# Encoder trunk: the split of the fourth in-projection slab goes to another slot and one step sooner, and half of the out-projection's weights is loaded later

## The reference

```
mod = silu(c) @ mod_w[l] + mod_b[l]              # six parts of 1024: shift, scale, gate, twice
h = rmsnorm(x, g) * (1 + scale) + shift
z = h @ w_in                                     # 2560 columns: a_val, a_gb, a_gc, b_gate, b_in, 512 each
y_a = a_gb * conv3(a_gc * a_val)
xr = conv4(b_in) + b
h_rec = rglru(xr, forward) + rglru(xr, reverse)  # sigmoid gates, a = exp(...), linear scan over the sequence
y_b = gelu(b_gate) * h_rec
x = x + gate * (concat(y_a, y_b) @ w_out)
x = x + gate2 * grouped_moe(...)                 # 16 experts, top 2
...
```

## Time and profile before

| | |
|---|---|
| runs of the kernel | 1388.5, 1387.87, 1386.01 us; median 1387.87 |
| the profiled execution's own time | 1388.95 us |
| its span, first to last instruction | 1387.2 us |
| busy: PE, DVE, ACT, POOL | 1278.2, 1033.7, 680.4, 164.0 us |
| mean granted clock of PE | 0.969 |
| out-projection of layer 0 starts | 201.48 us |

### The profile page before, as it was taken

How to read it: one execution, slowest core, us unless ns; L and a number is a source line. 1 busy time by engine, 2 the same in 40 slices (tenths; PEclk the granted TensorE clock), 3 DMA queues, 4 the chain that set the end, 5 groups by cost and what they waited for, 6 DMA issues and landing times.

```text
span 1387.2 us, 15640 instructions
## 1 busy us (share of the span) xinstructions
PE 1278.2 (92%) x5389; PEld 907.8 (65%) x5389; DVE 1033.7 (75%) x1415; ACT 680.4 (49%) x877; POOL 164.0 (12%) x169
## 2 busy tenths in 40 slices
PE   2999899989999999996899999999799999999876
PEld 2466765577777777753788854468777777777532
DVE  8679975477898888837766587856678898888253
ACT  3477402326667666614222167644366667666002
POOL 6000000010000000010000057710100000000200
PEclk9999999899999999999999999999899999999989
DMA  9727674257999999885465230022689999998651
GB/s 353 243 91 273 227 264 190 91 212 279 379 384 378 389 384 388 323 320 212 134 235 180 89 122 0 1 77 99 278 312 392 389 381 381 385 381 321 234 198 60
DMA packets 78116, 347.84 MB, mean 251 GB/s; under 512 B 12500, under 2 KB 12684, under 8 KB 69104
## 3 DMA queue, kind: packets, MB, share of 16 engines
q1 hardware_dynamic: 67184, 325.70, 62.7%
q0 software_dynamic: 7344, 16.68, 3.2%
q10 hardware_dynamic: 3536, 4.79, 0.9%
HBM read 334.15 MB, written 23.07 MB: 258 GB/s over the span
## 4 chain that ended last, share of the span: by engine, by line
PE 73%; DVE 13%; DMA 6%; ACT 4%; issue 3%; POOL 1%; SPq 0%; DVEq 0%; POOLq 0%; ACTq 0%
PE ps L1968 24%; PE ps L2101 8%; PE ps L1994 8%; PE ps L2001 6%; PE ps L1879 4%; DVE scratch L1054 3%; PE ps L1886 3%; PE ps L1954 2%; PE ps L1846 2%; DMA mod_ring<-y_rows,y_row 2%; PE ps L2145 2%; PE ps L2173 2%; PE ps L2159 2%; DMA x_res<-in_x_dram 1%; PE ps L1841 1%
## 5 line engine op out<-in xcount | busy, mean ns | idle before, releaser
L1968 PE MATMUL ps<-slab_ring_r,gate_rows_r 128*128 128x512 f32 x512 | 200.8, 392 | 0.0
L1476 DVE TENSOR_TENSOR slab_ring_r<-slab_ring,h_t_r 128x2048 fp32r<-128x2048 f32 x64 | 143.7, 2284 | 5.3 <-ACT h_t_r L858 5.3
L2101 PE MATMUL ps<-slab_ring_r 128*128 128x512 f32 x384 | 120.0, 394 | 6.3 <-DVE h_t_r L1111 6.3
L858 ACT ACTIVATE h_t_r<-slab_ring 128x2048 fp32r<-128x2048 f32 x64 | 118.7, 1903 | 0.0
L1994 PE MATMUL ps<-slab_ring,scratch 128*128 128x512 f32 x256 | 116.9, 600 | 1.5 <-ACT scratch L900 1.5
L1968 PEld LDWEIGHTS ps<-slab_ring_r,gate_rows_r 128*128 128x128 f32 x512 | 97.1, 190 | 18.5
L1968 PE MATMUL ps<-h_t_r,gate_rows_r 128*128 128x512 f32 x256 | 104.3, 407 | 4.9 <-DVE slab_ring_r L1476 4.9
L1968 PE MATMUL ps<-h_t_r,scratch_r 128*128 128x512 f32 x256 | 101.4, 396 | 0.0
L725 POOL TENSOR_SCALAR mod_ring<-mod_ring,row_rcp 128x512 f32<-128x512 f32 x48 | 76.9, 1614 | 204.7 <-DVE row_rcp L1732 204.6
L1476 DVE TENSOR_TENSOR slab_ring_r<-slab_ring,x_norm_r 128x2048 fp32r<-128x2048 f32 x32 | 73.1, 2287 | 19.3 <-ACT x_norm_r L858 19.3
L1476 DVE TENSOR_TENSOR slab_ring_r<-slab_ring,mod_ring_r 128x2048 fp32r<-128x2048 f32 x32 | 73.1, 2287 | 19.3 <-ACT mod_ring_r L858 19.3
(11 more groups left out here) (360 smaller groups left out, 2710.3 us busy)
## 6 DMA issues: line engine op xcount, KB each, us to landing
slab_ring<-in_expert_w_gate_dram SPq DMA_DIRECT2D x35, 2048.0 KB, 8.6
slab_ring<-in_expert_w_up_dram SPq DMA_DIRECT2D x35, 2048.0 KB, 10.1
slab_ring<-in_expert_w_down_dram SPq DMA_DIRECT2D x35, 2048.0 KB, 10.3
mod_ring<-in_mod_w_dram SPq DMA_DIRECT2D x40, 512.0 KB, 4.7
y_rows<-scratch SPq DMA_DIRECT2D x32, 512.0 KB, 10.5
slab_ring<-in_mod_w_dram SPq DMA_DIRECT2D x32, 512.0 KB, 4.8
slab_ring<-in_mod_w_dram SPq DMA_DIRECT2D x12, 1024.0 KB, 11.3
slab_ring<-in_w_qkv_dram SPq DMA_DIRECT2D x6, 2048.0 KB, 17.0
```

Source lines behind the costliest of these rows:

```text
L858: act.activation(top, w, ACT.Copy).then_inc(high_ready[c], 1)
L1476: tt_(rest, w, top.bitcast(F32), ALU.subtract).then_inc(low_ready[c], 1)
L1968: ins = pe.matmul(ps[:, bank, :], x, w, start=(kt == 0 and i == 0), stop=(kt == KT - 1 and i == 2))
L2101: ins = pe.matmul(ps[:, i % 6, :], x[:, kt, cut], y[:, k, :], start=(kt == 0 and n == 0), stop=(kt == KT - 1 and n == 2))
```

## The change

The high parts of slab 3 go to slot 0 of the ring, which is free once slab 0's four tiles are done, and are made one tile step sooner on ACT, behind tiles j = 1 and j = 2 in place of 2 and 3. Slab 4's high parts keep `HT_r`, which they now share with slab 2 only. The low parts of slab 3 are moved ahead in DVE's list. Slot 0 is then taken until z tile 15, so the first out-projection slab is loaded later, behind the second.

```diff
@@ in_split_of
-        top = ring_r[:, 5, :, :] if g == 1 else HT_r
+        top = {1: ring_r[:, 5, :, :], 2: HT_r, 3: ring_r[:, 0, :, :], 4: HT_r}[g]
@@ SP
         load_mod(4)
-        load_slab(("out", 0), w_out[:, :, 0:HALF])
         load_mod(5)
         sp.wait_ge(z_ready, 12)
         load_slab(("out", 1), w_out[:, :, HALF:D])
+        sp.wait_ge(z_ready, 16)
+        load_slab(("out", 0), w_out[:, :, 0:HALF])
         load_mod(6)
@@ ACT, high_in
-            if g > 2:
-                act.wait_ge(z_ready, 4 * (g - 1) + 2 * half + 2)
+            if g == 3:
+                act.wait_ge(z_ready, 4)
+            if g == 4:
+                act.wait_ge(z_ready, 10 + 2 * half)
@@ ACT, end of tile step j
-            if j >= 2:
-                high_in(3, j - 2)
+            if j in (1, 2):
+                high_in(3, j - 1)
@@ DVE
         gates_in(2)
+        low_in(3, 0)
         mod_acc(3, 6, 2)
         gates_out(2)
-        low_in(3, 0)
         mod_acc(4, 0, 3)
         gates_in(3)
+        low_in(3, 1)
         mod_acc(4, 3, 2)
         gates_out(3)
-        low_in(3, 1)
         mod_acc(4, 5, 3)
```

## The result

The changed kernel takes 1391.55 us (median of 20 runs, 1387.83 to 1395.75), the kernel before 1387.86 (20 runs, 1384.79 to 1391.09). The ratio is 1.0019 with a 95% interval of 1.0011 to 1.0028, that is 2.6 us slower (1.5 to 3.9). The medians differ by 3.7 us. The change made the kernel a little slower, by an amount that lies at the line of 0.2%.

What follows compares the result with a forecast made beforehand. The prediction took DVE's arrival at low_in(4, 1), then a race between PE and DVE, as the bound. DVE's order (2.21 us) and the second slab (1.47) sum to 3.68, giving 1387.87 + 3.7 = 1391.5 us; range 1388.0 to 1393.8.

Steps and rivals of the forecast that it cites:

- the sum: Likeliest case: DVE's 2.21 us and the second slab's 1.47 add to 3.68 us; chance 0.55, 0.49 of it to slower.
- Part 1: ACT: slab 3's high parts one tile step sooner fit its 5.13 us idle time; cost nothing, gain nothing.
- Part 2: DVE: low_in(3, 0) ahead of gates_out(2) delays ACT's j = 3 step, so DVE waits longer for ACT; +2.21 us.
- Part 3: PE: tile 14 no longer waits, its 4.3 us hole goes to before tile 16; gain nothing.
- Part 4: Transfer queue: the second out-slab ahead of load_mod(6)'s slices makes DVE wait 2.1 us; +1.47 us at the out-projection.
- The unknown: PE's clock may fall after 2.3 us pauses before tile 18 and the out-projection; taken as nothing, upper bound 1.7 us.
- B: Rival: load_mod(6)'s slices are not held up by the second slab, only DVE's order costs; +2.2 us, 1390.1; chance 0.16.
- C: Rival: PE's clock falls before the out-projection (1393.3), or slab 3 lands late for ACT's j = 2 step (1393.8); chance 0.13.
- D: Rival: no effect; ACT's step does not hold DVE and the slices come in time; 1387.9; chance 0.09.
- E: Rival: faster; PE decides, tile 14's 4.3 us wait and the slow clock carry to tile 19; 6.0 us, 1381.9; chance 0.07.

Runs made afterwards that it cites:

- e3: Changed kernel with DVE's old order restored and one out-projection slab moved behind load_mod(6); ratio to the kernel before 1.0000 (0.9987 to 1.0013).
- e1: Changed kernel with DVE's list put back in the old order, loads as changed; ratio to the kernel before 0.9998 (0.9980 to 1.0016).
- e7: Changed kernel with low_in(3, 1) ahead of gates_in(3) in place of behind it; ratio to the kernel before 1.0007 (0.9989 to 1.0025).
- e2: Changed kernel with one out-projection slab ahead of load_mod(6) and the other behind it, DVE's order as changed; ratio to the kernel before 1.0003 (0.9987 to 1.0018).
- e6: Changed kernel with out-slab ("out", 0) issued from ACT's queue after z tile 15, not from SP; ratio to the kernel before 1.0006 (0.9991 to 1.0021).
- changed_again: The changed kernel once more, with no edit, for a second profile; ratio to the kernel before 1.0026 (1.0010 to 1.0042).
- e4: Changed kernel with e2's edit, low_in(3, 0) ahead of gates_in(2) and low_in(3, 1) ahead of gates_in(3); ratio to the kernel before 0.9988 (0.9971 to 1.0005).
- e5: e4 with six mod_acc products ahead of gates_in(0) and low_in(2, 0) ahead of gates_out(0); ratio to the kernel before 0.9963 (0.9946 to 0.9981).
- e8: e5 with low_in(4, 1) moved ahead of mod_acc(5, 6, 2) and val(3); ratio to the kernel before 0.9978 (0.9964 to 0.9991).
- e5_again: The kernel of e5 run a second time, with no edit; ratio to the kernel before 0.9986 (0.9971 to 1.0000).

## Why the prediction was right

**Result.** 1391.5 was forecast and 1391.55 measured. That the two agree to 0.05 us is luck: timed again, the changed kernel's median lay 4.7 us over that of the kernel before (1393.27 against 1388.56) and not 3.7. What supports the sum are the terms, read in the traces. The case with the largest chance, the sum, is what happened. The ratio with its interval puts the loss at 1.5 to 3.9 us, which holds the 3.68 of the sum, near its upper end, but also values on the other side of the 0.2% line. That split of the chances can't be called confirmed; the medians alone are on the slower side.

**Part 1** (sooner high parts cost nothing): right. The slab landed near 112.5 against 112.4, and e3 shows no cost.

**Part 2** (2.21 us by DVE's order): right. The traces show 2.15 at `low_in(4, 1)` in absolute time and 2.22 as a distance; e1 and e7 take it away, each in another way, and e2 shows it alone. The waits were forecast as 1.16 and 2.4, and are 1.20 and 2.38.

**Part 3** (PE's hole moves to before tile 16, no gain): right, and in e1 and e3, where the longest of PE's waits is 2.8 us, the first distance is that of before with its 4.3. One number was off: the pause before tile 18 was to be 2.3 us and was 1.17. Behind the longer hole tile 16 began at the lower clock (0.50 from 174 to 178 us, where before had 0.58), and tiles 16 and 17 took 13.85 us (174.88 to 188.73) where before's took 12.75. The forecast had not counted that. That ate a part of the pause and delayed nothing, since tile 18 waits for DVE.

**Part 4** (1.47 us by the second slab): right. DVE's wait was 2.10 (2.1 forecast), the third slice was used by 195.82 (195.76), and PE waited for the last `gb`. e1 measures the term alone as 1.49; e2 and e6 take it away.

**The unknown**, PE's clock before the out-projection: the pause was 2.35 us, and the granted clock from 205 to 209 was 1.00. Nothing was lost, as taken, and that was luck too. Four runs had a pause of nearly this length there: the changed kernel 2.35 us, changed_again 2.32 and e7 2.39 kept the clock at 1.00, and e1 with 2.27 lost it, and with it the 1.70 us that the prediction gave as its upper bound.

**Rivals.** B (the slices overtake) is refuted by the 14.4 us from issue to landing and by e2. That a later transfer may complete before an earlier one doesn't mean that a small one passes 4 MB ahead of it, and here none did. C asked for a lower clock behind 205 or for a slab landing at 117.6; neither is there in the changed kernel, but e1 shows that C's clock was a real risk. For D, ACT's step does hold DVE. E asked that `low_in(4, 1)` start no later than before. That was not so here; e4, e5 and e8 met its condition by another order of DVE, and there the out-projection starts 1.5 to 4.1 us sooner than before (e4's 115.17 and e8's 112.60 against 116.65). E's full 6.0 us came in none of them.

**The profiled execution** was to take 1392.6, with a span of 1390.9. Its span was 1394.0; the 3 us more lie behind the out-projection's start and did not come back in changed_again.

## What to carry to other kernels

When an engine splits its time between a chain that another engine answers (here DVE's scan, ACT's next gates) and work that only has to be done some time, put that work ahead of the wait for the answer, not between the last result and the signal that starts the answer: the same two low parts of 2.2 us each cost 2.2 us behind the gates (e2) and gained 1.5 us ahead of them (e4). Ask of a large load not only whether it is needed late enough, but which small ones stand behind it in the queue. A hole on an engine off the last chain was worth nothing here: the changed kernel, e1 and e3 moved or cut PE's hole and gained nothing by it.

## What the runs showed of the hardware that was not expected

Pauses of nearly one length had both outcomes for TensorE's clock. Eight matmuls of 512 columns, of the same line, took 5.37 us behind a pause of 2.50 us in e1 and 3.67 in e5, in another tile step. Each of these rows is PE in order of time:

```profile
126.96 5.37 PE L1859 MATMUL ps<-scratch,gate_rows 128*128 128x512 f32 x8 [2.50 <-DVE scratch L1222]
```

```profile
108.15 3.67 PE L1857 MATMUL ps<-scratch,gate_rows 128*128 128x512 f32 x8 [2.50 <-DVE scratch L1221]
```

From 126 to 131 us the granted clock was 0.69 in e1 and 1.00 in the changed kernel, whose pause there was 2.43. The same kernel went both ways: in changed_again the pause at this place was 2.49 us, the eight took 5.37, and the granted clock over the same 5 us was 0.81. Nor does the length alone sort the outcomes: in e1 a pause of 2.27 us kept the clock before tile 18 (1.00 from 187 to 191) and one of 2.27 lost it before the out-projection (0.62), and in e5_again one of 2.52 kept it (3.67 us). Behind pauses of 2.76, 3.09 (e4) and 5.97 us (changed) PE ran at the lower clock. So the pause of 2.35 us before the out-projection lay among lengths that went either way, and a plan for such a pause should keep both outcomes.

The clock also fell with no pause at all. In the changed kernel PE goes from a series of 16 matmuls that write one column each straight into the out-projection again (its last two rows in PE's order of time, 218.96 and 222.55).

PE is busy for all of the 4 us from 222 to 226, and the granted clock there is 0.50 (last row of its table of stretches), the level of 1.2 GHz. Six matmuls took 5.47 us, 0.91 each, where 32 of the same took 13.97, 0.44 each, from 205.15 on at 1.00. This too went both ways: in e7 the same series stands there, the granted clock from 222 to 226 was 1.00, and the six took 2.82 us.
